# Attention by groups of eight heads inside the next block products, and the probabilities scaled on VectorE

## The chip, the cores and the metric

The kernel runs on one core of one Trainium2 chip. The metric is the device time of one execution in microseconds. Before the change it is 1536.22 us, the median of three runs (1534.34 to 1536.5). Everything is computed in float32.

## The reference

One sequence of 256 tokens with 1024 features runs through an mLSTM layer, an expert layer (16 experts, 32 tokens each), a gated linear attention layer, a second expert layer, and then a second block: attention with 16 heads of 64, and a gated feed-forward of width 2816 with a short causal convolution. The change concerns the attention. With 256 tokens there is one block of keys, so its code reduces to

```python
y = rms_norm_2(h, attn_norm)
q, k, v = split(y @ w_qkv)                    # 16 heads of 64 each
s = (q @ k^T) * 64 ** -0.5 + rel_bias[head, bucket(qpos - kpos)]
s = where(kpos <= qpos, s, NEG)
p = softmax(s)                                # per head, 256 x 256, lower triangle
h = h + (p @ v) @ w_o
y = rms_norm_2(h, ffn_norm)
h = h + conv_ffn(y, w_up, conv_w, conv_b, w_down)
```

## The kernel before

Five engines each run their own program, written out by hand in order, and meet at semaphores. `@block.sync` (SP) issues nearly all loads, `@block.gpsimd` (GpSimd, POOL in the profile) makes part of the weight sums, small loads and, in the attention, a part of the scaling; `@block.tensor`, `@block.scalar` and `@block.vector` are TensorE (PE), ScalarE (ACT) and VectorE (DVE).

**Weights.** All weights pass through a ring of nine slots of 2 MB (`SLOTS`, `ring_plan`). `ring_plan` gives each 2 MB tile the slot that came free first; `TILE_BEFORE` names the tile that must have been used before SP may load into it (`free`, L540, waits on `tile_used`). SP's loads are one queue in program order, so a load that waits holds all behind it. Tiles 206 and 207 are the last expert's; 208 to 213 are w_qkv, 214 and 215 w_o, 216 to 226 w_up, 227 on w_down. Before the change tile 215 (w_o's second) and 216 wait for 206 and 207, 217 to 222 for 208 to 213.

**Block products.** A projection of 256 tokens by 1024 columns is done as seven products of quarter blocks instead of eight (a Strassen-like scheme; `block_product`, L866). The products are numbered and run as 1, 2, 3, 6, 5, 7, 4. Product x of block u multiplies a block or sum of tokens with a block or sum of weights into the bank `BLOCK_BANKS[u][x]`. The sums of tokens are made by VectorE (`left_and_right_sums`, L1724); the sums of weights in three rounds: GpSimd `first_weight_sums` (L680; the instruction is L685), VectorE `second_weight_sums` (L1734; L1739), GpSimd `last_weight_sums` (L687; L694), each of them 512 columns wide, both inputs in SBUF. VectorE takes the results out of the banks in nine steps (`take_value`, L1756). Product 6 needs VectorE's second sums (`weights_summed[2]`), 7 and 4 need GpSimd's last ones. In a block of `TURNED` the weights are stationary and the result comes out with features on the partitions; else the tokens are stationary.

**Attention before.** V, Q and K are three blocks (`V_ATT, Q_ATT, K_ATT`), each for all 16 heads, one after the other. After the last product of K the eight pairs of heads go through: `scores` (L1262, products at L1273, into banks 2 to 5), on VectorE `maxima` (L2145; bias, causal mask and row maximum in one instruction, L2153), on ScalarE `exps` (L1583; exponent and row sums), on VectorE `scale` (L2158; reciprocal L2161, first 128 columns L2163), on GpSimd the other 256 columns (L789), on TensorE `turn_probs` (L1278) into banks 6 and 7, copies by ScalarE (L1607) and VectorE (L2179) into `probsT`, `values` (L1289), a copy of the heads by ScalarE (L1593), and the output block `O_ATT`. GpSimd loads the bias rows of four heads at a time (`bias_of`, L776) into two halves of `acc`; the first two loads are issued in front of `first_weight_sums(K_ATT)`, behind some loads for the feed-forward. The order at the end of the attention on TensorE is

```python
scores(0); scores(1)
for pair in range(AH // 2):
    if pair + 2 < AH // 2: scores(pair + 2)
    if pair >= 1: values(pair - 1)
    turn_probs(2 * pair); turn_probs(2 * pair + 1)
values(AH // 2 - 1)
```

Of the kernel before, what the change touches and what calls it, by code (L numbers as in the profile page):

```python
# [23 lines left out]
P = 128  # L24
# [53 lines left out]


def ring_plan():  # L80

    slots, before = [], []
    last = {s: None for s in range(SLOTS)}
    for n in range(T_DOWN + N_DOWN):
# [12 lines left out]
        s = min(range(SLOTS if layer is None else SLOTS + ROOM_SLOTS), key=freed)  # L97
# [4 lines left out]
    return slots, before  # L102


SLOT_OF, TILE_BEFORE = ring_plan()
# [35 lines left out]
def build_in(nc, t, out, ctx):  # L141
# [123 lines left out]
    aqk_t, av_t, prob_t, probT_t = rooms(16 * S, TT * D, 6 * 384, 768)  # L265
# [3 lines left out]
    probsT = probT_t.rearrange("p (b n) -> p b n", b=2)  # L269
# [36 lines left out]
    def right_block(i, odd, half):  # L306
# [10 lines left out]
    V_MLSTM, O_MLSTM, V_GLA, QK_GLA, O_GLA, V_ATT, Q_ATT, K_ATT, O_ATT = range(9)  # L317
# [3 lines left out]
    OUTPUTS, TURNED = (O_MLSTM, O_GLA, O_ATT), (QK_GLA, Q_ATT, K_ATT, *UPS)  # L321
# [3 lines left out]
        (0, 1, 2, 3), (4, 5, 6, 7), (0, 1, 2, 3), (2, 3, 0, 1), (4, 5, 6, 7), (4, 5, 6, 7), (0, 1, 2, 3), (4, 5, 6, 7),  # L325
# [4 lines left out]
    sums_room = {2: gb_t[:, :], 4: room[:, 6144:6144 + 2048]}  # L330
# [111 lines left out]
    p_first, p_second = sem("p_first"), sem("p_second")  # L442
# [96 lines left out]
    def _(sp):  # L539
        def free(n):  # L540

            if TILE_BEFORE[n] is not None:
# [78 lines left out]
        columns(T_QKV, t["w_qkv_2"][0], 2 * D, 2)  # L621
        columns(T_QKV + 2, t["w_qkv_2"][0], 0, 4)
# [20 lines left out]
    def _(pool):  # L643
# [158 lines left out]
    def _(pe):  # L802
# [452 lines left out]
        def attention():  # L1255
            keep_busy(13, PS[0])
            block_project(V_ATT, U_ATT)
            for u in (Q_ATT, K_ATT):
                for x in (1, 2, 3, 6, 5, 7, 4):
                    block_product(u, x)  # L1260

            def scores(pair):  # L1262
                if pair >= 2:
                    pe.wait_ge(max_done, 2 * pair - 2)
# [1083 lines left out]
```

## Time and profile before

| | us |
|---|---|
| median of 3 runs | 1536.22 |
| span of the profiled execution | 1531.2 |
| TensorE busy | 1270.1 (83%) |
| VectorE busy | 517.8 (34%) |
| GpSimd busy | 318.2 (21%) |
| ScalarE busy | 214.2 (14%) |
| V, Q and K, from the first product to the last | 1184.0 to 1260.7 |
| softmax and values | 1260.7 to 1291.0 |
| output block | 1291.0 to 1315.5 |

The profile is that of one execution, its times are microseconds from the start of the span. A row of a timeline gives the start, the duration, the engine, the line, the operation, output and inputs, and how many instructions are merged; in brackets the idle time before it and what ended it. Two matmul records stand for one float32 matmul. A duration of VectorE includes its filling and emptying, so the next instruction can start somewhat before it ends. The granted clock is given in shares of 2.4 GHz.

### The profile page before, as it was taken

To read this page: it belongs to the slowest core of one execution; us is meant where nothing else is said; L and a number is where in the kernel's file an instruction comes from. 1 tells how busy PE (TensorE), PEld (TensorE's weight loads), DVE (VectorE), ACT (ScalarE), POOL (GpSimd) and SP (SyncE) were. 2 spreads that over 40 slices of the span, in tenths; PEclk is the share of its full clock that TensorE was granted. 3 is DMA by queue.
4 is the path that set the end of the run, shared out by engine and by line. 5 is a ranking of instruction groups with operands and counts; after the bars stand their busy time and mean duration, and the time that the engine had idled before them with its cause. 6 is when DMAs were issued, how large, how long until landed. Compare 5 with 4: busy or idle time off the path is not lost.

```text
span 1531.2 us, 21562 instructions
## 1 busy us (share of the span) xinstructions
PE 1270.1 (83%) x9321; PEld 731.4 (48%) x9321; DVE 517.8 (34%) x980; ACT 214.2 (14%) x440; POOL 318.2 (21%) x274
## 2 busy tenths in 40 slices
PE   9998987668667668999896667677768998999998
PEld 7554533223223234865543223223324694799953
DVE  2457211001001006676411000000003546488894
ACT  1032100000000001351200000000001005212110
POOL 1404000000000004674100000000001566376700
PEclk9999999887889889999999888888799999999999
DMA  9938899999999999834799999999999973534100
GB/s 344 373 122 317 329 427 428 427 427 427 427 427 427 428 424 369 314 160 193 291 427 428 428 426 428 427 426 428 426 428 399 372 224 129 165 111 176 73 0 28
DMA packets 88286, 498.89 MB, mean 326 GB/s; under 512 B 8452, under 2 KB 31392, under 8 KB 63872
## 3 DMA queue, kind: packets, MB, share of 16 engines
q1 hardware_dynamic: 85728, 490.23, 78.9%
q0 software_dynamic: 2464, 7.29, 1.4%
q8 instruction: 74, 1.21, 0.3%
q14 instruction: 20, 0.16, 0.0%
HBM read 496.42 MB, written 1.07 MB: 325 GB/s over the span
## 4 chain that ended last, share of the span: by engine, by line
PE 50%; DMA 40%; DVE 6%; another core or an unknown queue 2%; issue 1%; ACT 1%; SPq 1%; DVEq 0%; POOL 0%
DMA weight_ring<-in_moe_w_down 20%; PE bank L891 13%; DMA weight_ring<-in_moe_w_up 10%; PE bank L894 7%; PE bank L1182 5%; PE bank L1361 4%; PE bank L857 3%; PE bank L1234 3%; PE bank L1247 3%; DMA phase_room<-in_moe_w_down 3%; DMA phase_room<-in_moe_w_gate 3%; DMA weight_ring<-in_moe_w_gate 3%; PE bank L1157 1%; PE bank L1330 1%
## 5 line engine op out<-in xcount | busy, mean ns | idle before, releaser
L1182 PE MATMUL bank<-weight_ring,x_tok 128*32 128x256 f32 x3328 | 231.2, 427 | 113.3 <-DMA weight_ring<-in_moe_w_up 93.3
L1182 PEld LDWEIGHTS bank<-weight_ring,x_tok 128*32 128x32 f32 x3328 | 112.1, 120 | 228.0 <-issue 92.4
L1234 PE MATMUL bank<-weight_ring,xT 128*32 128x512 f32 x864 | 134.4, 752 | 71.2 <-DMA weight_ring<-in_moe_w_down 64.7
L694 POOL TENSOR_TENSOR weight_ring<-weight_ring 128x512 f32<-128x512 f32 x112 | 154.9, 1414 | 133.6 <-PE bank L891 78.9
L2084 DVE TENSOR_TENSOR xT<-xT,bank 128x256 f32<-128x256 f32 x32 | 13.5, 421 | 463.6 <-PE bank L1182 463.6
L685 POOL TENSOR_TENSOR weight_ring<-weight_ring 128x512 f32<-128x512 f32 x56 | 75.1, 1373 | 457.7 <-DMA weight_ring<-in_w_qkv 442.1
L1247 PE MATMUL bank<-x_tok,xT 128*128 128x512 f32 x256 | 121.0, 616 | 0.0
L2089 DVE COPY x_tok<-bank 128x512 f32<-128x512 f32 x32 | 22.1, 691 | 247.8 <-PE bank L1234 247.8
L1234 PEld LDWEIGHTS bank<-weight_ring,xT 128*32 128x32 f32 x864 | 27.4, 124 | 150.3 <-DMA weight_ring<-in_moe_w_down 67.2
L720 POOL DMA_DIRECT2D phase_room<-in_gla_w_in x1 | 1.0, 965 | 435.1 <-PE bank L1234 435.1
L1247 PEld LDWEIGHTS bank<-x_tok,xT 128*128 128x128 f32 x256 | 47.5, 196 | 84.5 <-issue 84.5
L891 PE MATMUL bank<-xT,weight_ring 128*128 128x128 f32 x768 | 87.7, 275 | 0.0
L891 PEld LDWEIGHTS bank<-xT,weight_ring 128*128 128x128 f32 x768 | 86.8, 192 | 1.0 <-issue 1.0
L891 PE MATMUL bank<-acc,weight_ring 128*128 128x128 f32 x640 | 73.2, 275 | 0.2
L891 PEld LDWEIGHTS bank<-acc,weight_ring 128*128 128x128 f32 x640 | 72.2, 192 | 0.9 <-issue 0.9
L1182 PE MATMUL bank<-phase_room,x_tok 128*32 128x256 f32 x768 | 49.8, 408 | 24.3 <-DMA phase_room<-in_moe_w_up 17.8
L1739 DVE TENSOR_TENSOR weight_ring<-weight_ring 128x512 f32<-128x512 f32 x56 | 65.8, 1220 | 4.6 <-PE bank L891 3.7
L894 PE MATMUL bank<-weight_ring,xT 128*128 128x512 f32 x144 | 65.0, 596 | 2.2 <-issue 1.4
L857 PE MATMUL bank<-weight_ring,xT 128*128 128x512 f32 x128 | 59.0, 594 | 0.6 <-PE bank L857 0.6
L894 PE MATMUL bank<-weight_ring,acc 128*128 128x512 f32 x128 | 57.1, 597 | 1.1 <-DVE weight_ring L1739 1.1
L1557 ACT ACTIVATE xT<-bank 128x256 f32<-128x256 f32 x32 | 12.3, 383 | 274.7 <-PE bank L1209 274.7
L1182 PEld LDWEIGHTS bank<-phase_room,x_tok 128*32 128x32 f32 x768 | 25.3, 116 | 48.8 <-issue 17.5
(299 smaller groups left out, 1528.4 us busy)
## 6 DMA issues: line engine op xcount, KB each, us to landing
weight_ring<-in_moe_w_gate SPq DMA_DIRECT2D x52, 2048.0 KB, 49.7
weight_ring<-in_moe_w_up SPq DMA_DIRECT2D x52, 2048.0 KB, 49.5
weight_ring<-in_moe_w_down SPq DMA_DIRECT2D x52, 2048.0 KB, 49.4
phase_room<-in_moe_w_gate SPq DMA_DIRECT2D x12, 2048.0 KB, 48.3
phase_room<-in_moe_w_up SPq DMA_DIRECT2D x12, 2048.0 KB, 49.5
weight_ring<-in_w_up SPq DMA_DIRECT2D x22, 1024.0 KB, 10.9
phase_room<-in_moe_w_down SPq DMA_DIRECT2D x8, 2048.0 KB, 50.3
weight_ring<-in_gla_w_in SPq DMA_DIRECT2D x6, 2048.0 KB, 23.3
```

The lines of the kernel that those rows point to most:

```text
L685: nc.gpsimd.tensor_tensor(a, a, b, ALU.subtract).then_inc(weights_summed[1], 1)
L694: nc.gpsimd.tensor_tensor(b, a, b, ALU.subtract).then_inc(weights_summed[x], 1)
L857: last = mm(bank[:, :], xT[:, k, tt * P:(tt + 1) * P], w[:, k, :], start=(k == 0), stop=(k == KC - 1), skip_group_check=True)
L891: last = mm(bank[:, c * P:(c + 1) * P], w[:, k, c * P:(c + 1) * P], left[:, k], start=(first and c == 0), stop=(k == HALF - 1), skip_group ...
L894: last = mm(bank[:, :], left[:, k], w[:, k], start=first, stop=(k == HALF - 1), skip_group_check=True)
L1157: last = mm(PS[quarter % 2][:, at:at + P], x_perm[:, tt, k, :], sels[g][:, tt], start=(tt == 0), stop=(tt == TT - 1))
L1182: last = mm(bank[q * CAP:(q + 1) * CAP, 0:S], xinT[:, 4 * r + k, j * CAP:(j + 1) * CAP], w[k][:, q * S:(q + 1) * S], start=(r == 0 and k = ...
L1234: last = mm(PS[i][k * CAP:(k + 1) * CAP, :], hidT[:, 4 * r + k, :], w[k][:, i * 512:(i + 1) * 512], start=(r == 0), stop=(r == 1), skip_gr ...
L1247: last = mm(PS[4 + 2 * tt + i][:, :], selT[:, tt * P:(tt + 1) * P], exp_t[:, i * 512:(i + 1) * 512], start=False, stop=True, skip_group_ch ...
L1361: last = mm(PS[bank][:, :], left[:, p], w[:, r], start=(first and (i, r) == blocks[0]), stop=((i, r) == blocks[-1]), skip_group_check=True)
L1739: v.tensor_tensor(a, a, b, ALU.subtract).then_inc(weights_summed[2], 1)
L2089: v.tensor_copy(exp_t[:, 512:1024], PS[1][:, :]).then_inc(exp_dve, 1)
```

## The change

w_qkv is cut by heads: `QK_LOW` computes queries and keys of heads 0 to 7, `QK_HIGH` those of heads 8 to 15, and V comes last. The tiles are loaded in that order into the same slots as before. QK_LOW's products run alone. Between the products of QK_HIGH stand the scores and the turning of pairs 0 to 3, between those of V those of pairs 4 to 7; all eight `values` follow V's last product. The turned probabilities of all 16 heads are kept, in two ring slots that held the last expert's tiles (`HELD_SLOTS`, slots 1 and 2; 3072 columns for eight heads), and so are the sums of tokens of the three blocks (1024 columns each). These two slots take no tile from w_qkv on until the eighth w_up tile; tile 215 now waits for 208, 216 for 209, 217 to 221 for 210 to 214, 222 for 215, and 223 and 224 for the last copied head (`o_copied`). Scores use banks 4 and 5 only, so a pair's scores wait for the maxima of the pair before. GpSimd scales nothing; VectorE scales all 384 columns of a head, two heads at a time (`invert`). The first product of the output block waits for the copies of four pairs, the others for all.

```diff
-    V_MLSTM, O_MLSTM, V_GLA, QK_GLA, O_GLA, V_ATT, Q_ATT, K_ATT, O_ATT = range(9)
+    V_MLSTM, O_MLSTM, V_GLA, QK_GLA, O_GLA, QK_LOW, QK_HIGH, V_ATT, O_ATT = range(9)
...
     def tokens_sum(u, x):
+        if SUMS_OF[u] == 4:
+            at = 8 * 384 + 512 * ((x - 1) % 2)
+            return held[(x - 1) // 2][:, at:at + 512].rearrange("p (k s) -> p k s", s=P)
...
-            if TILE_BEFORE[n] is not None:
+            if TILE_BEFORE[n] == HELD:
+                sp.wait_ge(o_copied, AH // 2)
+            elif TILE_BEFORE[n] is not None:
...
# GpSimd
-        first_weight_sums(V_ATT)
-        last_weight_sums(V_ATT)
-        first_weight_sums(Q_ATT)
-        last_weight_sums(Q_ATT)
+        first_weight_sums(QK_LOW)
+        last_weight_sums(QK_LOW)
+        first_weight_sums(QK_HIGH)
         pool.wait_ge(tokens_ready, tokens_count(U_ATT, TT - 1))
...
         for g in range(2):
             bias_of(g)
-        first_weight_sums(K_ATT)
-        last_weight_sums(K_ATT)
-        for h in range(AH):
-            pool.wait_ge(inv_ready, h + 1)
-            c, pr = 2 * (h % 6), probs[:, h % 6]
-            nc.gpsimd.tensor_scalar(pr[:, P:P + S], pr[:, P:P + S], inv_prob[:, c + 1:c + 2], None, ALU.mult
-                                    ).then_inc(p_second, 1)
-            if h in (0, 3):
-                bias_of(2 + h // 3)
+        last_weight_sums(QK_HIGH)
+        bias_of(2)
+        first_weight_sums(V_ATT)
+        bias_of(3)
+        last_weight_sums(V_ATT)
         for u in (O_ATT, *UPS):
...
# TensorE
+            for u, first in ((QK_HIGH, 0), (V_ATT, 4)):
+                for x in (1, 2, 3, 6, 5, 7, 4):
+                    if u == V_ATT and x in (1, 2):
+
+                        pe.wait_ge(out_taken, 9 * QK_HIGH + 7 + x)
+                    block_product(u, x)
+                    if x == 1:
+                        if first:
+                            turn_probs(first - 1)
+                        scores(first)
+                    elif x == 3:
+                        scores(first + 1)
+                    elif x == 6:
+                        scores(first + 2)
+                    elif x == 5:
+                        turn_probs(first)
+                        scores(first + 3)
+                    elif x == 7:
+                        turn_probs(first + 1)
+                    elif x == 4:
+                        turn_probs(first + 2)
+            turn_probs(AH // 2 - 1)
+            pe.wait_ge(out_taken, 9 * (V_ATT + 1))
             for pair in range(AH // 2):
...
+                values(pair)
+            pe.wait_ge(o_copied, AH // 4)
+            block_product(O_ATT, 1)
             pe.wait_ge(o_copied, AH // 2)
-            block_project(O_ATT)
+            for x in (2, 3, 6, 5, 7, 4):
+                block_product(O_ATT, x)
...
# VectorE
+            def invert(pair):
+                dve.wait_ge(probs_exp, 2 * pair + 2)
+                c = 4 * (pair % 3)
+                v.reciprocal(inv_prob[:, c:c + 4], prob_sum[:, c:c + 4]).then_inc(inv_ready, 1)
+                dve.wait_ge(inv_ready, pair + 1)
+                for h in (2 * pair, 2 * pair + 1):
+                    c, pr = 2 * (h % 6), probs[:, h % 6]
+                    v.tensor_scalar(pr[:, 0:P], pr[:, 0:P], inv_prob[:, c:c + 1], None, ALU.mult)
+                    v.tensor_scalar(pr[:, P:P + S], pr[:, P:P + S], inv_prob[:, c + 1:c + 2], None, ALU.mult
+                                    ).then_inc(probs_scaled, 1)
...
+            for u, first in ((QK_HIGH, 0), (V_ATT, 4)):
+                take_value(u, 1, 1, 0, 0, None)
+                if first:
+                    copy_probs(first - 1)
+                maxima(first)
+                take_value(u, 2, 2, 0, 0)
+                second_weight_sums(u)
+                take_value(u, 3, 3, 0, 1, None)
+                maxima(first + 1)
+                invert(first)
+                take_value(u, 4, 6, 0, 1)
+                maxima(first + 2)
+                invert(first + 1)
+                take_value(u, 5, 5, 0, 1)
+                take_value(u, 6, 5, 1, 1, None)
+                maxima(first + 3)
+                invert(first + 2)
+                copy_probs(first)
+                take_value(u, 7, 7, 1, 1)
+                take_value(u, 8, 7, 1, 0, None)
+                invert(first + 3)
+                copy_probs(first + 1)
+                take_value(u, 9, 4, 1, 0, ALU.subtract)
+                copy_probs(first + 2)
+            copy_probs(AH // 2 - 1)
```

`maxima`, `scores` and `turn_probs` now handle a pair (two heads) per call; their instructions are the old ones.

## Rows read from the trace of the kernel before

**Rows 1.** The page, its first line.
```profile
span 1531.2 us, 21562 instructions
```

**Rows 2.** Windows: length, busy (x instructions) of PE, PEld, DVE, ACT, POOL, then PEclk, DMA.
```profile
1210.60:1260.70 50.10, 50.10 (x451) 49.98 (x449) 21.69 (x26) 0.00 (x0) 31.69 (x29) 1.00 0.82 264
1260.70:1291.00 30.30, 23.64 (x177) 15.09 (x176) 20.44 (x106) 20.26 (x80) 20.46 (x21) 0.89 0.54 174
```

**Rows 3.** Windows of the softmax's first 13 us, the same columns.
```profile
1261.00:1268.00 7.00, 3.68 (x30) 2.18 (x26) 4.97 (x31) 4.86 (x21) 3.24 (x4) 0.93 0.91 292
1268.00:1274.00 6.00, 6.00 (x32) 3.77 (x30) 3.39 (x16) 2.50 (x10) 3.62 (x5) 0.51 1.08 348
```

**Rows 4.** The chain that ended last, in order of time: start, us, what.
```profile
1268.31 1.58 PE bank L1273 x8
...
1274.22 0.80 PE bank L1299 x8
1275.03 0.81 PE bank L1286 x6
1275.84 0.91 PE bank L1273 x8
...
1291.01 24.50 PE bank L894 x56
```

**Rows 5.** Timeline of PE in the V block: start, us, engine, line, operation.
```profile
1184.03 3.67 PE L894 MATMUL bank<-weight_ring,xT 128*128 128x512 f32 x8 [0.30 <-issue]
...
1207.10 3.60 PE L894 MATMUL bank<-weight_ring,xT 128*128 128x512 f32 x8
1210.53 7.31 PE L891 MATMUL bank<-xT,weight_ring 128*128 128x128 f32 x64
```

**Rows 6.** Timeline of POOL around the loads that it issues.
```profile
1206.43 4.94 POOL L685 TENSOR_TENSOR weight_ring<-weight_ring 128x512 f32<-128x512 f32 x4
...
1230.97 1.56 POOL L768 DMA_DIRECT2D norm_rows<-in_conv_w  x3
...
1234.10 1.56 POOL L780 DMA_DIRECT2D acc<-bias_rows_dram  x2
```

**Rows 7.** Line L780, the four bias loads: from issue to landing.
```profile
DMA to landing us min/median/max: 6.2/7.1/7.7
```

**Rows 8.** Groups of VectorE instructions from 1150 us on: busy us, mean ns.
```profile
L1781 DVE TENSOR_TENSOR phase_room<-phase_room,bank 128x512 f32<-128x512 f32 x20 | 13.7, 684 | 18.4 <-PE bank L891 10.9 <-PE bank L894 7.3
L2153 DVE CUSTOM_DVE_ANT_0 phase_room<-bank,acc 128x128 f32<-128x128 f32 (+1 forms) x32 | 9.4, 352 | 1.8 <-PE bank L1273 1.8
L2163 DVE TENSOR_SCALAR phase_room<-phase_room,small 128x128 f32<-128x128 f32 x16 | 4.6, 288 | 0.6
L2179 DVE COPY phase_room<-bank 128x384 f32<-128x384 f32 x8 | 4.5, 558 | 5.2 <-PE bank L1286 4.8
```

**Rows 9.** Timelines, single instructions: VectorE with two SBUF inputs beside GpSimd's sums.
```profile
1219.68 1.27 POOL L694 TENSOR_TENSOR weight_ring<-weight_ring 128x512 f32<-128x512 f32 x1 [8.31 <-PE bank L891]
1219.73 1.76 DVE L1739 TENSOR_TENSOR weight_ring<-weight_ring 128x512 f32<-128x512 f32 x1 [0.20 <-PE bank L891]
...
1356.16 1.49 DVE L2199 SCALAR_TENSOR_TENSOR phase_room<-norm_rows,phase_room 128x255 f32<-128x255 f32 x1
1357.58 1.49 DVE L2199 SCALAR_TENSOR_TENSOR phase_room<-norm_rows,phase_room 128x255 f32<-128x255 f32 x1
```

**Rows 10.** Timelines, single instructions: VectorE's scalings (L2163) and GpSimd's (L789).
```profile
1264.72 1.01 POOL L789 TENSOR_SCALAR phase_room<-phase_room,small 128x256 f32<-128x256 f32 x1 [8.67 <-DVE small L2161]
1265.05 0.31 DVE L2163 TENSOR_SCALAR phase_room<-phase_room,small 128x128 f32<-128x128 f32 x1
...
1267.56 0.91 POOL L789 TENSOR_SCALAR phase_room<-phase_room,small 128x256 f32<-128x256 f32 x1
...
1269.01 0.29 DVE L2163 TENSOR_SCALAR phase_room<-phase_room,small 128x128 f32<-128x128 f32 x1
1269.07 1.01 POOL L789 TENSOR_SCALAR phase_room<-phase_room,small 128x256 f32<-128x256 f32 x1 [0.60 <-DVE small L2161]
```

More of the change, by code:

```diff
@@ L77 @@
 ONCE = SLOTS + ROOM_SLOTS
+T_HELD = T_UP + 2
+HELD = T_WO + 1.5
 def ring_plan():
-    slots, before = [], []
+    slots, before, held = [], [], []
     last = {s: None for s in range(SLOTS)}
@@ L96, in ring_plan @@
             continue
-        s = min(range(SLOTS if layer is None else SLOTS + ROOM_SLOTS), key=freed)
+        if n == T_QKV:
+            held = sorted(range(SLOTS), key=freed)[-2:]
+        elif n == T_HELD:
+            last.update((s, HELD) for s in held)
+        s = min((s for s in range(SLOTS if layer is None else SLOTS + ROOM_SLOTS)
+                 if s not in held or n >= T_HELD), key=freed)
         key = s if s < SLOTS else (layer, s)
@@ L101, in ring_plan @@
         last[key] = n
-    return slots, before
-SLOT_OF, TILE_BEFORE = ring_plan()
+    return slots, before, held
+SLOT_OF, TILE_BEFORE, HELD_SLOTS = ring_plan()
 def constants():
@@ L262, in build_in @@
     inv_sum_r = small[:, 140:142]
-    aqk_t, av_t, prob_t, probT_t = rooms(16 * S, TT * D, 6 * 384, 768)
+    aqk_t, av_t, prob_t = rooms(16 * S, TT * D, 6 * 384)
+    held = [ring[:, s * TILE:(s + 1) * TILE] for s in HELD_SLOTS]
     aqk = aqk_t.rearrange("p (n s) -> p n s", s=S)
@@ L620, in _ @@
         experts(1)
-        columns(T_QKV, t["w_qkv_2"][0], 2 * D, 2)
-        columns(T_QKV + 2, t["w_qkv_2"][0], 0, 4)
+        for half in range(2):
+            columns(T_QKV + 2 * half, t["w_qkv_2"][0], 512 * half, 1)
+            columns(T_QKV + 2 * half + 1, t["w_qkv_2"][0], D + 512 * half, 1)
+        columns(T_QKV + 4, t["w_qkv_2"][0], 2 * D, 2)
         out_columns(T_BLOCK[O_ATT], t["w_o_2"][0])
@@ L1769, in take_value @@
                     scale = None if j else DK ** -0.5
[L1770 to L1773 removed]
+                elif u in (QK_LOW, QK_HIGH):
+                    at = 8 * j + 4 * (u - QK_LOW)
+                    to = aqk[:, at:at + 4, tokens]
+                    if j == 0:
+                        to, scale = to[:, :, ::-1], -AD ** -0.5
                 else:
@@ new lines, in attention, with maxima @@
+            first_values(QK_LOW)
+            middle_values(QK_LOW)
+            last_values(QK_LOW)
+            def maxima(pair):
+                for h in (2 * pair, 2 * pair + 1):
+                    dve.wait_ge(s_done, h + 1)
+                    dve.wait_ge(bias_landed[(h // 4) % 2], 16 * (h // 8 + 1))
+                    if h >= 6:
+                        dve.wait_ge(pt_done, h - 5)
+                    b, c, pr = PS[4 + h % 2], 2 * (h % 6), probs[:, h % 6]
+                    for at, n, j in ((0, P, c), (P, S, c + 1)):
+                        last = v.tensor_tensor_reduce(pr[:, at:at + n], b[:, at:at + n],
+                                                      bias_flip[:, (h // 4) % 2, h % 4, S - n:S], 1.0, 3e38,
+                                                      ALU.add, ALU.min, neg_max[:, j:j + 1])
+                    last.then_inc(max_done, 1)
```

144 lines of the change are left out of this document (49 added, 95 removed).

## The prediction

> **What bounds the kernel now.** I read the page first: the span is 1531.2 us [rows 1]. The three timed runs have a median of 1536.22 us, so some 5.0 us lie around the profiled span; every term below is a difference against the profiled execution and is put on that median. Then the windows of the attention [rows 2]: from 1210.6 to 1260.7 two blocks run with TensorE busy 50.10 of 50.10 us, and from 1260.7 to 1291.0 the softmax and the values have it busy 23.64 of 30.30 us, at a granted clock of 0.89. Cut finer [rows 3], the first 7 us hold 3.68 us of work, and behind them the clock is 0.51 for 6 us, the lower of its two levels (1.2 GHz). The chain of waits [rows 4] shows what a group costs: scores of a pair 1.58 us in the slow stretch, but 0.91 a few us later; turning a pair's probabilities 0.81, values of a pair 0.80. So eight pairs need 8 x (0.91 + 0.81 + 0.80) = 20.2 us, and about 10 us of the 30.3 are waits and half clock. All around it TensorE is the bound. The change is worth at most those 10 us; the question is what waits it brings.
>
> **TensorE's work.** From the first V product at 1184.03 [rows 5] to the end of the output block (1291.01 + 24.50 = 1315.5, [rows 4]) are 131.5 us. A product costs 3.43 us with tokens stationary (the start of row 1207.10 to 1210.53, [rows 5]) and 50.1 / 14 = 3.58 us turned [rows 2]. After the change: QK_LOW takes V's place, 26.6 us and 0.5 for the dearer products, 27.1; QK_HIGH 25.1; V 24.0; scores and turns 8 x 1.72 = 13.8; values 6.4; output block 24.5. That is 120.9 us, **10.6 less**. Its first product waits for four copied pairs only, which hides the last copies. The scores between other products are the same instructions; nothing shows a cost of switching, and I bound it by 0 and 0.3 us for each of the 16 groups (half of what the slow scores cost more), and take 0.
>
> **Loads.** Two ring slots are held from the last expert on. w_o's second tile and the first w_up tile now wait for QK_LOW's tiles (about 1211) instead of the last expert's; they are wanted at 1282 and 1307. Later w_up tiles wait for QK_HIGH, V and w_o, always one block or more ahead; at the 264 GB/s of the first of rows 2 a 2 MB tile needs 8 us. The held slots come back for the eighth and ninth w_up tiles, behind waits on SP's queue that are later anyway. Cost 0, covered by 25 us of block work. The copies of turned probabilities (0.56 us, [rows 8]) keep their size; only their place changes.
>
> **The bias rows.** GpSimd issues conv rows, gains and the first two bias loads after QK_HIGH's first sums, which end at 1206.43 + 4.94 = 1211.4 [rows 6]. The first bias load stands 3.13 us behind the first conv row (1230.97 to 1234.10), so it is issued at 1214.5, and it lands after 6.2 to 7.7, median 7.1 us [rows 7]: 1221.6. Now VectorE wants it at 1215.2, right after scores(0), where before 20 us of products lay between. Behind this wait stand value 2 and the second weight sums, which product 6 needs. From 1221.6: maxima of a pair 1.1 (9.4 / 8 = 1.2, overlapping a little, [rows 8]), value 0.6 (0.684, the next starts sooner), weight sums 4.6 (two at 0.6, two held by GpSimd to 1.7, as in rows 9), value 0.6, maxima 1.1: 1229.7. TensorE could have had scores(2) at 1227.3. **Cost 2.5 us** (1.6 to 3.1 by the landings). Bias 2 and 3 are issued over 10 us before V's maxima ask for them: 0.
>
> **VectorE's scalings.** Two blocks each get 8 maxima (4.5 us), 16 scalings, 4 reciprocals (0.9) and 4 copies (2.1) beside some 10.5 us of values and sums. The scaling of 128 columns takes 0.288 us [rows 8] and its successor can start 0.2 us later; for 256 columns no row exists on VectorE: lower bound the 0.288, upper bound GpSimd's 1.00 [rows 10]; I take 0.35 (0.27 to the next start), as the maxima of 128 and 256 columns average only 0.352. So an inversion (two heads) costs 0.2 + 2 x 0.47 = 1.15 us and VectorE is busy some 23 of 32 us. If nothing holds these scalings, no further wait arises and the total is 10.6 - 2.5 = 8.1 us faster.
>
> But GpSimd runs weight sums at just that time: eight last sums follow VectorE's second sums, then four first sums of the next block, 15 us out of 32. [Rows 9] show what two-input VectorE instructions suffer beside them: started 0.05 us after a GpSimd sum, a sum of 512 columns (0.684 from a bank, [rows 8]) took 1.76, ending 0.54 after it; and two neighbours without a wait between them took 1.49 each, starting 1.42 apart: they take turns, one GpSimd instruction for one of VectorE. Is a one-input scaling from SBUF subject to this? [Rows 10]: GpSimd's scaling took 0.91 where no VectorE scaling overlapped its start and 1.01 where one began 0.06 us before it; so it is for 14 of the 16 against two. Sharing is there. Against it speaks one VectorE scaling that began 0.33 us into a GpSimd scaling and took 0.31, not held. No row has a VectorE scaling beside a two-input GpSimd sum. Bounds: 0 and a whole GpSimd sum (1.27 us) for each scaling. I take the upper one, because the held ones in rows 9 stood beside the same GpSimd instruction and the free one did not.
>
> The Trainium skill (GPSIMD Engine Reference, section 8, Key points) says that GpSimd contends with VectorE instructions in a 2-port perf mode or with two SBUF inputs; VectorE: DVE Perf Modes, section Mode 2×_2P, puts fp32 tensor_scalar from SBUF to SBUF into that mode. By that rule the sum is the held one; by the free instruction of rows 10 alone it would be the other.
>
> Held, the chain from 1229.7 is: inversion 0 with three to four held scalings 4.7; value 4 0.6; maxima 1.1 (1236.1; scores(3) wait 1.1 us for it); inversion 1 with four held 5.5; values 5 and 6 1.3; maxima 1.1; inversion 2, GpSimd now done, 1.2; copy 0.5: 1245.8. TensorE reaches the second half of turn_probs(1), which needs that copy's bank, at 1241.0 and waits 4.8. QK_HIGH ends at 1250.6 instead of 1245.0: 5.6 us. In V the same order from value 3 (1265.5) takes 17.7 us; TensorE waits 1.0 at scores(7) and 4.1 before turn_probs(5): 5.1 us. Total 10.7 us, so 8.1 - 10.7 = **2.6 us slower**. Each of the two long waits is longer than the 3.3 us idle in all that preceded the stretch at clock 0.51 [rows 3]; that stretch held four groups, the first dearer by 1.58 - 0.91 = 0.67 [rows 4], 2.7 us for four. I count one such stretch; none and two are the bounds. Sum: 1536.2 + 2.6 + 2.7 = **1541.5 us**.
>
> **Rivals.**
> A, the forecast: scalings take turns with GpSimd's sums. Own range 1536 to 1546.
> B, faster: the scalings run free, or VectorE keeps the port for its four neighbours and waits once. Then 1536.2 - 8.1 = 1528.1 (1526.5 to 1531). For it: the free instruction of rows 10 and that a scaling holds its port for a small part of its 0.288 us. Against: rows 9 and the 0.1 us of GpSimd. It decides against A from the point where a scaling beside a sum costs less than about 0.8 us more; there the wait at turn_probs(1) no longer eats the 8.1.
> C, in between: the holds are real but fewer, or the bias rows land later. Each us of landing beyond 7.1 costs 1 us straight, so B with a landing of 12 us gives 1533, with 15 us 1536: the loads of two 2 MB tiles are released at 1211 and compete with it, though the four of rows 7 met such traffic too. A without a clock dip and with three quarters of the holds gives 1536. I take 1535.5 (1532 to 1538.5).
> D, that nothing is hidden since TensorE is the bound: excluded, as 6.7 us without TensorE work are in rows 2.
>
> **Chances.** A 0.51, B 0.35, C 0.14. The measurement can tell 0.2%, 3.1 us. Faster (below 1533.1): B 0.34 and a quarter of C, 0.37. Same: most of C and 0.05 of A, 0.15. Slower (above 1539.3): the rest of A and little of C, 0.48. The range of 1527 to 1545.5 leaves out B's lower end and A's upper end, some 0.15 in all, and holds C.
>
> **What would show it.** Right: VectorE's first maximum idle until a bias load lands, about 6 us; scalings beside GpSimd sums of 1.2 to 1.5 us, those without at 0.29 and 0.35; TensorE idle 4 to 5 us before turning the probabilities of pair 1 and of pair 5; a clock near 0.5 behind one of them; values in 6.4 us; the output block as before. Wrong: scalings at 0.3 to 0.4 everywhere, which is B; maxima idle over 8 us, or turns waiting for bias loads, which is C; products longer than 3.6 us at full clock, or TensorE waiting for a tile of w_o or w_up, would be none of them.

## The result, and the profile after

The changed kernel took 1543.31 us (median of 4 runs, 1542.39 to 1545.26), the kernel before 1535.28 us (4 runs on the same chip, 1533.21 to 1536.5). The ratio is 1.0056, with a 95% interval of 1.0042 to 1.0070: slower by over 0.2%. The profiled span went from 1531.2 to 1540.9 us. Forecast were 1541.5 us and this sign, by case A.

To see where it went I use one stretch in every kernel of this study: from the start of the first product of QK_LOW (V in the kernel before) to the start of the output block. Its beginning varies by up to 3 us between executions of any kernel (the expert stage ahead waits for DMAs); its length is the change's own. Before it is 1291.01 - 1184.03 = 106.98 us [rows 4, 5], after 1300.71 - 1183.73 = 116.98 us: **10.0 us more**, which is the whole change of the span (9.7). From the end of the output block to the end of the span both need 215.8 us.

The timeline of TensorE in the changed kernel (start us, us, engine line op, in brackets the idle time ahead and what ended it). L1286 are scores, L1298 turns of probabilities, L905 and L908 block products, L1311 the values:

```profile
1215.23 3.84 PE L905 MATMUL bank<-xT,weight_ring 128*128 128x128 f32 x32
1218.90 3.74 PE L905 MATMUL bank<-weight_ring 128*128 128x128 f32 x32
1225.77 0.93 PE L1286 MATMUL bank<-phase_room 64*128 64x128 f32 x8 [3.13 <-DVE small L2187]
1227.06 5.24 PE L905 MATMUL bank<-weight_ring 128*128 128x128 f32 x32 [0.37 <-DVE weight_ring L1773]
1232.64 0.93 PE L1286 MATMUL bank<-phase_room 64*128 64x128 f32 x8 [0.33 <-DVE small L2187]
...
1238.88 0.93 PE L1286 MATMUL bank<-phase_room 64*128 64x128 f32 x8 [0.89 <-DVE small L2187]
...
1244.33 0.55 PE L1298 MATMUL bank<-consts,phase_room 128*128 128x128 f32 x3 [0.76 <-DVE phase_room L2200]
1249.23 0.87 PE L1298 MATMUL bank<-consts,phase_room 128*128 128x128 f32 x3 [4.35 <-DVE weight_ring L2205]
1249.89 5.68 PE L905 MATMUL bank<-xT,weight_ring 128*128 128x128 f32 x32
...
1278.69 0.93 PE L1286 MATMUL bank<-phase_room 64*128 64x128 f32 x8 [0.82 <-DVE small L2187]
...
1287.41 0.52 PE L1298 MATMUL bank<-consts,phase_room 128*128 128x128 f32 x3 [3.84 <-DVE weight_ring L2205]
1287.77 5.29 PE L908 MATMUL bank<-weight_ring,xT 128*128 128x512 f32 x8
...
1294.90 5.88 PE L1311 MATMUL bank<-weight_ring,phase_room 128*64 128x256 f32 x64
1300.71 7.13 PE L908 MATMUL bank<-weight_ring,xT 128*128 128x512 f32 x16
```

Against [rows 4, 5] the reader sees three places that cost. **One**: 3.13 us idle before scores(1), then a product of 5.24 us instead of 3.84 (granted clock 0.75 from 1225.7 to 1232.4). **Two**: 4.35 us before the second head of turn_probs(1), then a product of 5.68 instead of 3.74. **Three**: 3.84 us before the second head of turn_probs(5), then a product of 5.29 instead of 3.60. The windows of TensorE's waits and of what followed (columns: PE, PEld, DVE, ACT, POOL busy, then PE's granted clock, DMA share, GB/s):

```profile
1244.30:1249.90 5.60, 1.22 (x7) 1.01 (x8) 5.36 (x20) 2.23 (x9) 0.77 (x1) 0.75 0.10 31
1249.90:1256.10 6.20, 6.20 (x40) 6.20 (x40) 2.62 (x8) 0.16 (x1) 0.00 (x0) 0.67 0.17 59
1256.10:1283.60 27.50, 26.65 (x97) 12.51 (x95) 21.41 (x46) 6.78 (x27) 15.70 (x12) 1.00 0.48 153
1283.60:1287.40 3.80, 0.00 (x0) 0.02 (x1) 3.66 (x17) 2.23 (x9) 0.00 (x0) 1.00 0.00 0
1287.40:1293.70 6.30, 6.29 (x17) 2.99 (x17) 3.31 (x9) 0.28 (x1) 0.00 (x0) 0.73 0.00 0
```

The clock was at 1.00 through 27 us of full work, and at 0.67 and 0.73 in the 6 us behind each long wait: part of each of those windows ran at the lower level (1.2 of 2.4 GHz), as in [rows 3]. VectorE was busy 3.66 of the 3.80 us for which TensorE stood still. What held VectorE is in its groups, 1205 to 1326 us (busy us, mean ns, then its idle time):

```profile
L2199 DVE TENSOR_SCALAR phase_room<-phase_room,small 128x128 f32<-128x128 f32 x16 | 13.3, 831 | 0.3
L2200 DVE TENSOR_SCALAR phase_room<-phase_room,small 128x256 f32<-128x256 f32 x16 | 11.9, 747 | 0.0
L2187 DVE CUSTOM_DVE_ANT_0 phase_room<-bank,acc 128x128 f32<-128x128 f32 x16 | 4.5, 283 | 9.6 <-DMA acc<-bias_rows_dram 9.3 <-PE bank L1286 0.3
```

The scaling of [rows 8], 288 ns in the mean, now takes 831, and the first maximum sat 9.3 us waiting for a bias load. The means hide two kinds: 18 of the 32 scalings took 0.28 to 0.35 us, 13 stood beside GpSimd's sums (twelve took 0.60 to 1.38 us, one 5.07), and one took 0.60 beside a DMA issue of GpSimd. Single instructions of both engines show the turns (L713 and L704 are GpSimd's last and first weight sums):

```profile
1273.02 1.26 POOL L713 TENSOR_TENSOR weight_ring<-weight_ring 128x512 f32<-128x512 f32 x1
1273.06 1.37 DVE L2200 TENSOR_SCALAR phase_room<-phase_room,small 128x256 f32<-128x256 f32 x1
1274.25 1.31 POOL L713 TENSOR_TENSOR weight_ring<-weight_ring 128x512 f32<-128x512 f32 x1
1274.36 1.29 DVE L2199 TENSOR_SCALAR phase_room<-phase_room,small 128x128 f32<-128x128 f32 x1
1275.52 1.26 POOL L713 TENSOR_TENSOR weight_ring<-weight_ring 128x512 f32<-128x512 f32 x1
1275.56 1.37 DVE L2200 TENSOR_SCALAR phase_room<-phase_room,small 128x256 f32<-128x256 f32 x1
1276.85 0.68 DVE L1816 TENSOR_TENSOR phase_room<-phase_room,bank 128x512 f32<-128x512 f32 x1
...
1286.26 0.28 DVE L2199 TENSOR_SCALAR phase_room<-phase_room,small 128x128 f32<-128x128 f32 x1
```

Each scaling beside a sum ends just after that sum; the value at 1276.85, with one input from a bank and one from SBUF, isn't held beside the next sum (0.68 us, as in [rows 8]); and the scaling of 1286.26, behind GpSimd's last sum, takes 0.28. This is the pattern of [rows 9], now on scalings.

### The profile page after: what moved, and what is told of

Same layout as the page of the kernel before. It is cut to its first block, busy times and chain, and to the rows that moved or that the text cites. A ratio compares the mean times of both kernels' runs of the same rounds, so it can differ in the third digit from the quotient of the medians.

```text
span 1540.9 us, 21544 instructions
## 1 busy us (share of the span) xinstructions
PE 1270.4 (82%) x9321; PEld 735.0 (48%) x9321; DVE 532.9 (35%) x988; ACT 215.4 (14%) x440; POOL 302.9 (20%) x258
## 4 chain that ended last, share of the span: by engine, by line
PE 46%; DMA 40%; DVE 7%; issue 2%; another core or an unknown queue 2%; POOL 1%; ACT 1%; SPq 0%; DVEq 0%; POOLq 0%
DMA weight_ring<-in_moe_w_down 24%; PE bank L905 10%; PE bank L908 7%; DMA weight_ring<-in_moe_w_up 6%; PE bank L1196 5%; PE bank L1391 4%; PE bank L1261 4%; PE bank L871 3%; PE bank L1248 3%; DMA phase_room<-in_moe_w_down 3%; DMA phase_room<-in_moe_w_gate 3%; DMA weight_ring<-in_moe_w_gate 3%; PE bank L1171 1%; PE bank L1360 1%
## 5 line engine op out<-in xcount | busy, mean ns | idle before, releaser
L713 POOL TENSOR_TENSOR weight_ring<-weight_ring 128x512 f32<-128x512 f32 x112 | 155.6, 1419 | 170.2 <-PE bank L905 66.5
L704 POOL TENSOR_TENSOR weight_ring<-weight_ring 128x512 f32<-128x512 f32 x56 | 75.4, 1378 | 457.4 <-DMA weight_ring<-in_w_qkv 442.2
L905 PE MATMUL bank<-xT,weight_ring 128*128 128x128 f32 x768 | 90.1, 279 | 0.3 <-issue 0.3
L905 PEld LDWEIGHTS bank<-xT,weight_ring 128*128 128x128 f32 x768 | 88.9, 196 | 1.4 <-issue 1.3
L905 PE MATMUL bank<-acc,weight_ring 128*128 128x128 f32 x640 | 73.2, 276 | 0.2
L905 PEld LDWEIGHTS bank<-acc,weight_ring 128*128 128x128 f32 x640 | 72.2, 192 | 0.9 <-issue 0.9
L908 PE MATMUL bank<-weight_ring,xT 128*128 128x512 f32 x144 | 66.7, 609 | 1.4 <-issue 1.1
L908 PE MATMUL bank<-weight_ring,acc 128*128 128x512 f32 x128 | 57.1, 597 | 1.1 <-DVE weight_ring L1773 1.1
```

Of the source, the lines that this page charges most:

```text
L704: nc.gpsimd.tensor_tensor(a, a, b, ALU.subtract).then_inc(weights_summed[1], 1)
L713: nc.gpsimd.tensor_tensor(b, a, b, ALU.subtract).then_inc(weights_summed[x], 1)
L905: last = mm(bank[:, c * P:(c + 1) * P], w[:, k, c * P:(c + 1) * P], left[:, k], start=(first and c == 0), stop=(k == HALF - 1), skip_group ...
L908: last = mm(bank[:, :], left[:, k], w[:, k], start=first, stop=(k == HALF - 1), skip_group_check=True)
```

## The experiments

The theory (1): the loss is made of holds (VectorE's scalings waiting for GpSimd's sums), of the bias rows' landing, and of the half clock behind both. Rivals: VectorE's own load (2), the bias rows alone (3), the clock alone (4); the expectations name two more, ScalarE as the bound (5) and a hold of any form (6). Each kernel was timed beside the kernel before on the same chip. "Stretch" is the length defined above.

| kernel | us | ratio to before (95%) | stretch us |
|---|---|---|---|
| changed | 1543.31 | 1.0056 (1.0042 to 1.0070) | 116.98 |
| small_sums | 1529.12 | 0.9971 (0.9960 to 0.9982) | 101.39 |
| bias_early | 1538.46 | 1.0031 (1.0020 to 1.0042) | 110.53 |
| act_bias_early | 1523.28 | 0.9938 (0.9925 to 0.9952) | 96.38 |
| accum_bias_early | 1524.08 | 0.9941 (0.9927 to 0.9954) | 96.19 |
| act_late_bias | 1528.06 | 0.9968 (0.9957 to 0.9979) | 102.31 |
| busy_wait | 1544.67 | 1.0075 (1.0061 to 1.0088) | 117.47 |
| busy_wait_9 | 1539.51 | 1.0044 (1.0031 to 1.0056) | 112.99 |
| sums_first | 1536.97 | 1.0028 (1.0016 to 1.0039) | 109.31 |
| vector_scales_alone | 1536.88 | 1.0026 (1.0016 to 1.0036) | 110.06 |
| vector_sum_form_alone | 1535.58 | 1.0017 (1.0008 to 1.0026) | 108.29 |

The kernel before had a median of 1535.28 us beside the changed one, of 1532.79, 1532.80 and 1533.21 us beside the others, and a stretch of 106.98. A stretch comes from one execution.

**GpSimd's sums made small.** The kernel leaves out 511 of the 512 columns of these sums.

```
                 a, b = weight_block(u, 0, 1)[:, k], weight_block(u, 0, 0)[:, k]
+                if u in (V_ATT, O_ATT):
+                    a, b = a[..., 0:1], b[..., 0:1]
...
                     a, b = weight_block(u, 1, 1)[:, k], weight_block(u, second, 0)[:, k]
+                    if u in (QK_HIGH, V_ATT):
+                        a, b = a[..., 0:1], b[..., 0:1]
```

> The changed kernel, in which GpSimd's weight sums of the two softmax stretches (the last sums of QK_HIGH and V, the first sums of V and the output block) take 1 column of 512, in the same number and with the same waits; the weights' sums are so left out of the computation. Theory (VectorE's scalings and GpSimd's two-input sums take turns): all 32 scalings fall to 0.28 and 0.35 us, VectorE's second weight sums to some 0.6 us, the waits of 4.35 us before turn_probs(1) and 3.84 us before turn_probs(5) go down to 0 to 0.5 us, with them the waits before scores(3) and scores(7) (1.7 us together) and both stretches at half clock behind them (3.6 us); together 10 to 14 us less than the 1543.3 of the changed kernel: 1529.5 to 1533.5 (the bias rows' wait stays). Rival 2 (VectorE has too much of its own to do there): scalings fall, but the two waits keep over 3 us each, and the time stays over 1540. Rival 3 (the bias rows' late landing is the whole loss): the same time as the changed kernel, 1543, as the wait for them is not touched.

The stretch fell by 15.6 us and the time to 0.9971 of before. The 0.76, 4.35 and 3.84 us are gone from TensorE's timeline, and so are the scores' waits of 0.89 and 0.82; the first place stayed (3.06 us, then a product of 5.44). The group of VectorE's scalings:

```profile
L2203 DVE TENSOR_SCALAR phase_room<-phase_room,small 128x128 f32<-128x128 f32 x16 | 4.5, 284 | 0.3
L2204 DVE TENSOR_SCALAR phase_room<-phase_room,small 128x256 f32<-128x256 f32 x16 | 6.0, 377 | 0.0
```

The same instructions of the same shapes went from 831 and 747 ns to 284 and 377 when nothing but GpSimd's column count changed (377 and not 350, since two of them stood beside a DMA issue of GpSimd and took 0.56 and 0.60). Rivals 2 and 3 fall for this kernel. Expected were 10 to 14 us; by the ratios it is (1.0056 - 0.9971) x 1533 = 13.0. VectorE's own two-input weight sums were relieved as well (four in 2.49 us instead of 4.64), so this kernel alone doesn't say how much is the scalings'; accum_bias_early below does.

**The bias rows early.**

```
         first_weight_sums(QK_LOW)
+        pool.wait_ge(relb_stored, 16)
+        pool.wait_ge(tr_done, 4 * (U_ATT + 1))
+        for g in range(2):
+            bias_of(g)
         last_weight_sums(QK_LOW)
...
-        for g in range(2):
-            bias_of(g)
         last_weight_sums(QK_HIGH)
```

> The changed kernel, with the loads of bias rows 0 and 1 issued by GpSimd between the first and the last sums of QK_LOW, over 20 us earlier. All theories: the first maximum no longer waits for a DMA (9.3 us of VectorE idle, 3.13 us before scores(1), some 2 us more of TensorE's behind it). Theory: the chain to turn_probs(1) begins some 5 us earlier, GpSimd's last sums too (they follow VectorE's second sums), so the holds stay: scalings of 1.3 us, and 4 us of waiting before turn_probs(1) and (5); time 4 to 6 us less than 1543.3, 1537.5 to 1539.5. Rival 3 (the bias rows are the whole loss): the waits of TensorE before turn_probs(1) go too, and the time falls by 9 us or more, to 1534 or below. Rival 2: as the theory.

Stretch 6.45 us less; time by the ratios 3.8 us less (some 2.7 us either way), where 4 to 6 had been expected. VectorE's first maximum waits 0.16 us. The holds stayed, with the waits of 4.23 and 3.84 us, so the bias rows are a part of the loss and not the whole of it.

**The scalings on ScalarE, bias rows early.** This version beats both kernels. `f` is ScalarE's activation, here used as a plain scaling.

```
+            def scale_probs(pair):
+                act.wait_ge(inv_ready, pair + 1)
+                for h in (2 * pair, 2 * pair + 1):
+                    c, pr = 2 * (h % 6), probs[:, h % 6]
+                    f(pr[:, 0:P], pr[:, 0:P], ACT.Identity, scale=inv_prob[:, c:c + 1])
+                    f(pr[:, P:P + S], pr[:, P:P + S], ACT.Identity, scale=inv_prob[:, c + 1:c + 2]
+                      ).then_inc(probs_scaled, 1)
...
-                    v.tensor_scalar(pr[:, 0:P], pr[:, 0:P], inv_prob[:, c:c + 1], None, ALU.mult)
-                    v.tensor_scalar(pr[:, P:P + S], pr[:, P:P + S], inv_prob[:, c + 1:c + 2], None, ALU.mult
-                                    ).then_inc(probs_scaled, 1)
```

> The changed kernel with the bias rows early (as in bias_early) and with the 32 scalings on ScalarE (Identity with a scale for each partition) in place of VectorE, the reciprocals left on VectorE. Theory: ScalarE's scalings are not held by GpSimd (0.3 to 0.5 us each), VectorE keeps no one-input operation beside the sums but the values, no wait over 1 us is left in the two blocks and the clock stays high: 1543.3 - 5 (bias) - 10 (holds and clock) = 1528, range 1525 to 1532, faster than the kernel before (1535.3). Rival 2: as the theory, since VectorE is relieved of the same work. Rival 5 (ScalarE becomes the bound: 16 exponentials with 16 scalings a block): waits of TensorE before turn_probs stay 2 us or more and the time is over 1534.

1523.28 us, 0.9938 of the kernel before: 9.5 us faster than it, where 7 (1528) had been expected. ScalarE's timeline beside GpSimd's sums:

```profile
1228.93 0.39 ACT L1625 ACTIVATE phase_room<-phase_room,small 128x128 f32<-128x128 f32 x1
1229.22 0.49 ACT L1626 ACTIVATE phase_room<-phase_room,small 128x256 f32<-128x256 f32 x1
```

ScalarE's scalings are dearer than VectorE's free ones and none of the 32 is held (0.39 to 0.50 us each). From QK_LOW's second product on, ahead of which every kernel waits (0.96 us here, 0.91 in the kernel before), TensorE's only wait left in the stretch is 0.34 us, so rival 5 falls. Its 96.38 us are, but for these two waits, the length of the work: the prediction's 120.9 us less the output block's 24.5 give 96.4.

**VectorE again, in the form that also adds up.** Does the load on VectorE matter, or only the form of the instruction?

```
-                    v.tensor_scalar(pr[:, 0:P], pr[:, 0:P], inv_prob[:, c:c + 1], None, ALU.mult)
+                    v.tensor_scalar(pr[:, 0:P], pr[:, 0:P], inv_prob[:, c:c + 1], None, ALU.mult, ALU.add,
+                                    accum_out=small[:, 100 + c:101 + c])
```

and the same for the 256 columns.

> The changed kernel with the bias rows early and with the 32 scalings still on VectorE, but in the form that also adds its results up (the sums go to unused columns). The Trainium skill (VectorE: DVE Perf Modes, sections Mode 2x_2P and on which ops grab the shared pair in SBUF) says that only the form without a sum takes both read ports. Theory in its narrow form (it is the scaling's second port that collides with GpSimd's sums): the scalings take longer by themselves, 0.36 us for 128 and 0.49 us for 256 columns plus some 0.1 us for reading the sum, but none is held; the two long waits of TensorE (4.23 and 3.84 us in bias_early) fall to 0 to 1 us and the half clock goes; against the kernel before 6 to 10 us less (ratio 0.993 to 0.996). Rival 6 (any VectorE read and write of SBUF beside a GpSimd sum is held): scalings of 1.3 us stay and the ratio is that of bias_early, 1.003, or worse. Rival 2 (VectorE is too full): scalings are free but the waits stay over 3 us, as VectorE gets some 7 us more of its own work in the two blocks; ratio over 1.000.

```profile
L2201 DVE TENSOR_SCALAR_CACHE_REDUCE phase_room<-phase_room,small 128x256 f32<-128x256 f32 x16 | 7.6, 476 | 0.0
L2199 DVE TENSOR_SCALAR_CACHE_REDUCE phase_room<-phase_room,small 128x128 f32<-128x128 f32 x16 | 5.5, 345 | 0.3
```

Each scaling takes 0.06 to 0.13 us more than a free one of the plain form, but they are the same beside GpSimd's sums as away from them (0.34 to 0.35 and 0.47 to 0.48 us, all 32), and the two long waits are gone: 96.19 us, 0.9941. So neither VectorE nor its load was the trouble in this order of work, only a form that waits for GpSimd; rivals 2 and 6 fall. This is the exact test of the rule of the Trainium skill that the expectation names (it stands in SBUF — State Buffer, Who interferes with whom), and it came out so for all 32 instructions: the plain form was held, the form that writes out its accumulator never. Against bias_early only the form of the scalings differs, and the stretch is 14.3 us shorter.

**The bias rows' price without holds.** ScalarE scales, bias rows as in the change (the diff is that of act_bias_early without the moved loads).

> The changed kernel with the 32 scalings on ScalarE and the bias rows loaded where the change has them. It gives the price of the bias rows alone, without any hold. Theory: the stretch from the first product of QK_LOW to the end of the output block was 120.7 us with both repairs and 134.9 with the bias rows alone; here it is 120.7 and the wait of the bias rows, 5.0 to 6.5 us (TensorE idle 3.1 before scores(1), a half-clock product 6 behind it, and 0.5 to 1.5 at scores(3)): 126 to 127.5 us, against the kernel before 3 to 4.5 us less (ratio 0.997 to 0.998). If the bias rows' wait were hidden once the holds are gone, the ratio would be 0.994 as with both.

Stretch 102.31 us, 5.93 more than with the rows early; ratio 0.9968, at the edge of the 0.997 to 0.998 expected. The wait isn't hidden once the holds are gone.

**TensorE kept busy through the waits.**

```
             for h in (2 * pair, 2 * pair + 1):
+                if h % 8 == 3:
+                    keep_busy(15, PS[1])
                 pe.wait_ge(probs_scaled, h + 1)
```

> The changed kernel with 15 matmuls more (about 0.25 us each, into a free bank) before the second head of turn_probs(1) and of turn_probs(5), so that TensorE works through the two long waits of 4.35 and 3.84 us. This measures what the half clock behind the waits costs. Theory: product 4 of QK_HIGH falls from 5.68 to 3.6 us, product 4 of V from 5.29 to 3.5 us, 3.6 us in all, so 1539.7 (1538.5 to 1541.5, as the added matmuls may outlast the waits by some tenths). Rival 4 (the clock is most of the loss): 6 us or more less, 1537 or below, because turns and scores of other stretches speed up too. If the products stay at over 5 us although TensorE is busy, the clock has another cause, and the time stays 1543 or above.

A miss: 1544.67 us. The filler took 6.64 us for 15, since one takes 0.44 us and not 0.25, and outlasted both waits; what followed was indeed at full clock. So I ran nine:

> As busy_wait, with 9 added matmuls in place of 15: one takes 0.44 us (6.64 us for 15), not the 0.25 that I had reckoned with, so the 15 outlasted the waits by 2.0 and 2.5 us and gave back the 4.0 us that the full clock behind them saved. Nine take 4.0 us and end with the waits. Theory: products 4 of QK_HIGH and V stay at 3.7 and 3.6 us, the stretch from QK_LOW's first product to the output block's end is 141.5 - 4.0 = 137.5 us (to 138.5), and the time 3 to 4 us under the changed kernel's: ratio to the kernel before 1.0030 to 1.0040. Rival 4 (clock is most of the loss): ratio under 1.001.

```profile
1244.80 4.05 PE L823 MATMUL bank<-consts 128*128 128x256 f32 x18
1249.32 0.52 PE L1300 MATMUL bank<-consts,phase_room 128*128 128x128 f32 x3 [0.46 <-DVE weight_ring L2207]
1249.67 3.74 PE L905 MATMUL bank<-xT,weight_ring 128*128 128x128 f32 x32
...
1281.24 4.05 PE L823 MATMUL bank<-consts 128*128 128x256 f32 x18
1285.26 0.52 PE L1300 MATMUL bank<-consts,phase_room 128*128 128x128 f32 x3
1285.61 3.60 PE L908 MATMUL bank<-weight_ring,xT 128*128 128x512 f32 x8
```

The products behind the waits are back at 3.74 and 3.60 us, the stretch is 3.99 us shorter (from the first head of turn_probs(1) on 3.94; ahead of it both kernels agree within 0.1). By the ratios it is 1.8 us, with some 2.9 either way, so the times alone don't show a gain, and the ratio is a little outside the 1.0030 to 1.0040 expected; the traces, one execution of each, show it product by product. With the waits filled and nothing else changed, the half clock behind places two and three is worth 4.0 us in the traces, and the slow product of place one stayed (5.09 us). The clock is a part of the loss, and rival 4 (most of it) falls.

**One part of the change alone.** The kernel before, with VectorE in GpSimd's place for the 256 columns:

```
-            pool.wait_ge(inv_ready, h + 1)
-            c, pr = 2 * (h % 6), probs[:, h % 6]
-            nc.gpsimd.tensor_scalar(pr[:, P:P + S], pr[:, P:P + S], inv_prob[:, c + 1:c + 2], None, ALU.mult
-                                    ).then_inc(p_second, 1)
...
+                v.tensor_scalar(pr[:, P:P + S], pr[:, P:P + S], inv_prob[:, c + 1:c + 2], None, ALU.mult
+                                ).then_inc(p_second, 1)
```

> The kernel before with one part of the change alone: VectorE scales the 256 later columns, which GpSimd did, in the old order of attention, where GpSimd has no weight sums to make beside the softmax but those of the output block. Theory (only the company of GpSimd's sums makes a scaling dear): most scalings take 0.28 and 0.35 us, those that fall beside first sums of the output block 1.3; the second half of a head's probabilities is there 0.6 us sooner and VectorE is busy 16 x 0.27 = 4.3 us more in 30; the time is 0 to 3 us less than before (ratio 0.998 to 1.000). Rival 2 (VectorE's own load decides): 2 to 4 us more (ratio 1.001 to 1.003).

Slower by 0.26%, against the 0 to 3 us less that I expected: a miss, and a ratio in the range that I had given to rival 2. Most scalings are free, but the timelines of GpSimd and VectorE show this:

```profile
1270.01 0.75 POOL L780 DMA_DIRECT2D acc<-bias_rows_dram  x1 [4.68 <-DVE small L2149]
1270.78 4.93 POOL L685 TENSOR_TENSOR weight_ring<-weight_ring 128x512 f32<-128x512 f32 x4
1270.94 4.86 DVE L2159 TENSOR_SCALAR phase_room<-phase_room,small 128x128 f32<-128x128 f32 x1
1275.72 0.34 DVE L2160 TENSOR_SCALAR phase_room<-phase_room,small 128x256 f32<-128x256 f32 x1
```

In the kernel before, GpSimd's scalings kept its four first sums for the output block back until 1288.13. Relieved of them, it makes the sums 17 us sooner, in the middle of the softmax, and one scaling of VectorE is held for 4.86 us (TensorE idle for 3.37). An engine with less to do moved its work to where it hurt. Then the same in the form that isn't held:

> As vector_scales_alone (the kernel before, VectorE scales all columns), but in the form of accum_bias_early that also adds up. There a single scaling of 128 columns, begun 0.16 us after the first of four GpSimd sums for the output block (which start 17 us earlier, since GpSimd has nothing else to do), took 4.86 us, and TensorE stood idle for 3.37 us. Theory: no scaling is held any more (0.35 and 0.48 us each), the 3.4 us go and the half-clock groups behind them too: 4 to 6 us under vector_scales_alone, ratio to the kernel before 0.998 to 1.000. Rival 2 (VectorE's load made vector_scales_alone slow): as this form is dearer by 2.2 us in all, the ratio is 1.003 or more.

No scaling is held (0.35 and 0.48 us through all four sums), but the stretch falls by only 1.8 us and the ratio to 1.0017, where 0.998 to 1.000 had been expected; the intervals of the two overlap. A second miss, and here rival 2 is right in its place: from the fourth pair on, TensorE turns a pair every 3.3 us (1276.71, 1280.02, 1283.32), in the kernel before every 2.6 (1277.58, 1280.21, 1282.84), and VectorE is busy 6.48 of the 6.62 us of two pairs, in the kernel before 4.88 of 5.25. In the old order the softmax stands alone and VectorE has no slack for more work; in the new one the block products beside it give that slack.

**The sums ahead of a load.** In bias_early a scaling beside V's first sums took 5.09 us; here these sums come before the load of bias rows 2.

```
+        first_weight_sums(V_ATT)
         bias_of(2)
-        first_weight_sums(V_ATT)
         bias_of(3)
```

> bias_early with GpSimd's four first sums of V ahead of its load of bias rows 2, so that they begin 0.8 us sooner, right behind the last sums of QK_HIGH. In bias_early the scaling at 1234.70 began 0.06 us before the first of the four (which followed a DMA issue), and was held through all of them, 5.09 us. If what matters is that a scaling comes in the midst of a running sum, as in the V block, where they took turns (0.62, 1.37, 1.28, 1.37 us), then it is now the same here, with the same total: the wait before the second half of turn_probs(1) stays 3.5 to 4.5 us and the ratio 1.003, as in bias_early. If the hold of 5 us stays, it belongs to these sums and not to their start. Neither outcome touches the theory that the holds are the loss.

That scaling is now one of a row of turns, as in V:

```profile
1235.22 0.61 DVE L2199 TENSOR_SCALAR phase_room<-phase_room,small 128x128 f32<-128x128 f32 x1
1235.76 1.37 DVE L2200 TENSOR_SCALAR phase_room<-phase_room,small 128x256 f32<-128x256 f32 x1
1237.06 1.29 DVE L2199 TENSOR_SCALAR phase_room<-phase_room,small 128x128 f32<-128x128 f32 x1
1238.26 1.37 DVE L2200 TENSOR_SCALAR phase_room<-phase_room,small 128x256 f32<-128x256 f32 x1
```

The wait before the second half of turn_probs(1) is 3.83 us, as expected, and the 0.79 us before its first half are gone; the stretch is 1.2 us shorter than in bias_early. The ratio of 1.0028 is the same as there within the intervals.

## Why the prediction was right, and which terms were off

Taken apart by the runs, the stretch of the changed kernel is 96.4 us of work and 20.6 of waits and slow clock: 6.45 for the bias rows (changed less bias_early; 5.93 where nothing is held), 14.15 for the holds and what follows (bias_early less act_bias_early). Of the 14.15, TensorE's waits in bias_early are 0.46 + 0.79 + 4.23 + 0.83 + 3.84 = 10.15, and the 4.0 left are the half clock, as busy_wait_9 gave. The prediction had 15.9: 2.5, 10.7 and 2.7.

- **TensorE's work, 10.6 less**: 106.98 - 96.38 = 10.6 in act_bias_early. The sum came out to a tenth, its parts didn't. From start to start the 13 products of QK_HIGH and V that follow scores(0) took 46.7 us against 45.5, some 0.1 us each for standing between other work, which I had put at 0 of 0 to 0.3. Scores and turns took 12.7 against 13.8 and the values 5.8 against 6.4; a last wait of 0.34 gave a part of it back. That these errors cancelled is luck.
- **Loads, 0**: no wait of TensorE for w_o or w_up in the stretch, and none that the change brought behind it.
- **The bias rows, 2.5 us**: the step with the largest error, 6.45 measured. The issue was right (1214.5 forecast, 1214.20 in fact), the landing wasn't. The chain of waits after:

```profile
1214.20 10.14 DMA acc<-bias_rows_dram
```

  10.14 us instead of the 7.1 of [rows 7], 3.0 us straight. Case C had named why it might (the two 2 MB tiles released at 1211); that this was the reason isn't shown. In bias_early the first two loads are issued at 1191.72 into the same traffic (DMA share 1.04 and 367 GB/s from 1196 to 1202, against 1.03 and 370 from 1215.3 to 1222.6 in the changed kernel), and its four landed in 4.0 to 8.7 us; in act_bias_early and sums_first, which load them as early, the slowest took 10.3 and 10.2. The rest is a consequence that I left out: TensorE's 3.13 us before scores(1), followed at once by 0.37 and 0.33, bring a product at 5.24 us in place of 3.84, a third slow place.
- **VectorE's scalings, free 0.29 and 0.35**: 0.28 and 0.34 to 0.35. The value taken for 256 columns, for which no row stood in the trace, was right.
- **The holds, 10.7 us of TensorE's waits**: 0.89 and 0.76 + 4.35 in QK_HIGH (forecast 1.1 and 4.8), 0.82 and 3.84 in V (1.0 and 4.1): 10.66. The four forecast waits add up to 11.0, of which 10.7 went into the sum. The choice of the upper bound, a whole GpSimd sum for each scaling, was the step that decided the sign, and it held for the scalings that stood wholly beside sums (1.28 to 1.38 us each). By the free instruction of [rows 10] the forecast would have been B, 1528.1 us; that row stood beside a one-input operation of GpSimd and said nothing on its two-input sums.
- **The half clock, one stretch of 2.7 us**: two stretches, 4.0 us (busy_wait_9). I had two as the upper bound and chose one; [rows 3] had shown no more. The second wait, 3.84 us, was enough as well, and so was the bias rows' 3.13 us, whose slow product is in the term above.
- **Sum**: 5.3 us forecast, 10.0 in the stretch, 8.0 by the medians of the runs. The interval of the ratio, 6.4 to 10.7 us, holds the last two and not the first: the forecast of 1541.5 came nearer to the measured 1543.3 than its terms deserve, since it was put on a median of 1536.2 that a fourth run brought to 1535.3.

Of the signs listed, most of A's appeared: dear scalings beside sums and cheap ones away from them, TensorE idle before pairs 1 and 5 (4.35 and 3.84 us), a slow clock behind (behind both), and the output block as before (24.35 us); the values were quicker than listed. One of C's appeared too: a first maximum idle for over 8 us (9.3). A and C weren't rivals but terms of one sum, and I had joined C's late landing only to B.

## What to carry to other kernels

Before giving VectorE a plain scaling in SBUF, look at what GpSimd does at that time: if it is a run of two-input sums, each such instruction can cost a whole sum. With another form (one that adds up as well) or on ScalarE, and with the bias rows loaded earlier, the schedule that lost 8 us gains 9; with the bias rows late it gains 5. A transfer's median landing isn't a bound where the consumer stands right behind it: issue it a stage earlier. And a wait costs more than its length where TensorE's clock falls behind it; here 8 us of waits brought 4 us of slow products.

## What the runs showed that I had not expected

A scaling of 128 columns can be held through four GpSimd sums in a row: 5.07 us in the changed kernel, 5.09 in bias_early, 4.86 in vector_scales_alone. In all three the first of the four sums had followed a DMA issue of GpSimd, and began within 0.16 us of the scaling (0.03 and 0.06 us after it, 0.16 before it):

```profile
1238.20 0.77 POOL L798 DMA_DIRECT2D acc<-bias_rows_dram  x1
1238.95 5.07 DVE L2199 TENSOR_SCALAR phase_room<-phase_room,small 128x128 f32<-128x128 f32 x1
1238.98 1.28 POOL L704 TENSOR_TENSOR weight_ring<-weight_ring 128x512 f32<-128x512 f32 x1
...
1243.94 0.34 DVE L2200 TENSOR_SCALAR phase_room<-phase_room,small 128x256 f32<-128x256 f32 x1
```

The Trainium skill (SBUF — State Buffer, Who interferes with whom) has the one that issues first keep the port and the other wait for the whole instruction; by the records, the scaling of 1238.95 began first and waited, and for four instructions. Where a scaling began 0.7 us into a running sum, the two engines took turns (sums_first and the V block). Nearness of the starts alone can't be it, as scalings in the midst of such turns begin 0.04 us behind a sum (1273.06) and wait for that one only; whether the DMA issue ahead or the idle port at the start makes the difference wasn't separated. From the reciprocal ahead of them to the value behind them, four scalings took 5.9 us where one was held through all four sums (1238.74 to 1244.66) and 4.5 us where they took turns (1278.56 to 1283.09). In the stretch, sums_first is 1.2 us shorter than bias_early; its sums also begin 0.8 us sooner, so the two aren't separated.

GpSimd's DMA issues hold a scaling too. In the changed kernel the scaling of 1248.02 took 0.60 us beside the issue of 1247.76, which took 0.77; in small_sums the only two scalings that weren't free, 0.56 us at 1231.22 and 0.60 us at 1240.66, stood beside the issues of 1230.92 and 1240.40, 0.77 us each. All three ended 0.09 us after the issue.
